# Gate and up units of three feed-forward stages: the two state halves in one 512-column product

## What is computed

```python
def _swiglu(h, w_gate, w_up, w_down):
    return (jax.nn.silu(h @ w_gate) * (h @ w_up)) @ w_down

for layer in range(DEPTH):                       # DEPTH = 2
    h = _rmsnorm(x, ffn1_norm[layer])
    x = x + 0.5 * _swiglu(h, ffn1_w_gate[layer], ffn1_w_up[layer], ffn1_w_down[layer])
    ...
    h = _rmsnorm(x, ffn2_norm[layer])
    x = x + 0.5 * _swiglu(h, ffn2_w_gate[layer], ffn2_w_up[layer], ffn2_w_down[layer])
```

## Time and profile before

| | |
|---|---|
| median of 3 runs | 1725.09 us (1724.85 to 1726.63) |
| the profiled execution's own time | 1727.27 us |
| its span, first to last instruction | 1725.4 us |
| mean granted PE clock | 0.993 of 2.4 GHz |
| PE / PEld / DVE / ACT / POOL busy | 96% / 88% / 66% / 46% / 14% |
| HBM traffic | 328 MB read, 191 GB/s over the span |

### The profile page before, as it was taken

How to read it: one execution, slowest core, us unless ns; L and a number is a source line. 1 busy time by engine, 2 the same in 40 slices (tenths; PEclk the granted TensorE clock), 3 DMA queues, 4 the chain that set the end, 5 groups by cost and what they waited for, 6 DMA issues and landing times.

```text
span 1725.4 us, 30270 instructions
## 1 busy us (share of the span) xinstructions
PE 1658.2 (96%) x12336; PEld 1523.0 (88%) x12336; DVE 1137.1 (66%) x1385; ACT 791.2 (46%) x959; POOL 233.9 (14%) x300
## 2 busy tenths in 40 slices
PE   3999899999999999999999999999999999999998
PEld 2998799988987999889998978999899999889997
DVE  7877887888677444675657886555655557555554
ACT  1655433346445343453445656343544345553433
POOL 3000100000000000068946200000000004000000
PEclk8999999999999999999999999999999999999999
DMA  9954778784644655455554424555465555335552
GB/s 320 360 199 166 250 278 315 274 288 135 217 171 150 198 190 189 155 160 194 178 187 147 148 100 154 194 180 185 154 212 170 194 179 174 112 127 194 184 194 82
DMA packets 221391, 330.23 MB, mean 191 GB/s; under 512 B 6311, under 2 KB 183048, under 8 KB 221310
## 3 DMA queue, kind: packets, MB, share of 16 engines
q1 hardware_dynamic: 206112, 276.91, 48.0%
q0 software_dynamic: 14800, 52.06, 8.6%
q10 hardware_dynamic: 398, 0.11, 0.0%
HBM read 327.97 MB, written 1.09 MB: 191 GB/s over the span
## 4 chain that ended last, share of the span: by engine, by line
PE 82%; DVE 8%; ACT 4%; DMA 3%; issue 2%; SPq 0%; ACTq 0%; DVEq 0%; POOL 0%
PE bank L2380 41%; PE bank L2422 23%; PE bank L2410 7%; DVE s_wL L1871 2%; ACT s_wH L1504 2%; DVE s_late L1889 1%; PE bank L2392 1%; DMA s_raw<-in_w_in_ab 1%; DMA s_mix<-in_w_ada 1%; PE bank L2538 1%; PE bank L2530 1%; PE bank L2529 1%; DMA s_late<-in_w_ada 1%; PE bank L2479 1%; DVE s_mix L2083 0%
## 5 line engine op out<-in xcount | busy, mean ns | idle before, releaser
L1871 DVE TENSOR_TENSOR s_wL<-s_raw,s_wH 128x2048 fp32r<-128x2048 f32 x254 | 586.4, 2313 | 306.8 <-ACT s_wH L1504 306.2
L2380 PE MATMUL bank<-s_hH,s_wH 128*128 128x256 f32 x2240 | 636.9, 284 | 10.5 <-DVE s_hL L1919 5.2
L2380 PE MATMUL bank<-s_hH,s_wL 128*128 128x256 f32 x2240 | 634.5, 283 | 0.0
L2380 PE MATMUL bank<-s_hL,s_wH 128*128 128x256 f32 x2240 | 634.5, 283 | 0.0
L1504 ACT ACTIVATE s_wH<-s_raw 128x2048 fp32r<-128x2048 f32 x254 | 484.2, 1907 | 153.5 <-PE bank L2422 115.5
L2380 PEld LDWEIGHTS bank<-s_hH,s_wH 128*128 128x128 f32 x2240 | 430.3, 192 | 15.9 <-issue 11.6
L2380 PEld LDWEIGHTS bank<-s_hL,s_wH 128*128 128x128 f32 x2240 | 430.4, 192 | 2.3 <-issue 0.2
L2380 PEld LDWEIGHTS bank<-s_hH,s_wL 128*128 128x128 f32 x2240 | 430.4, 192 | 0.0
L2422 PE MATMUL bank<-s_wH,s_aH 128*128 128x512 f32 x488 | 192.1, 394 | 2.4 <-DVE s_aL L2089 2.4
L2422 PE MATMUL bank<-s_wL,s_aH 128*128 128x512 f32 x488 | 191.2, 392 | 0.0
L2422 PE MATMUL bank<-s_wH,s_aL 128*128 128x512 f32 x488 | 190.4, 390 | 0.0
(11 more groups left out here) (456 smaller groups left out, 2130.6 us busy)
## 6 DMA issues: line engine op xcount, KB each, us to landing
s_raw<-in_w_ffn_in SPq DMA_DIRECT2D x44, 1024.0 KB, 5.8
s_raw<-in_ffn_w_gate SPq DMA_DIRECT2D x44, 1024.0 KB, 5.1
s_raw<-in_ffn_w_up SPq DMA_DIRECT2D x44, 1024.0 KB, 5.1
s_raw<-in_ffn_w_down SPq DMA_DIRECT2D x44, 1024.0 KB, 4.8
s_late<-in_w_ada POOLq DMA_DIRECT2D x20, 2048.0 KB, 10.2
s_raw<-in_w_ffn_out SPq DMA_DIRECT2D x22, 1024.0 KB, 5.0
s_raw<-in_w_in_ab SPq DMA_DIRECT2D x12, 1024.0 KB, 11.5
s_raw<-in_w_in_cd SPq DMA_DIRECT2D x12, 1024.0 KB, 6.3
```

The source lines that it names most:

```text
L1871: TTn(wL[:, slot, :], raw[:, slot, :], wH[:, slot, :].bitcast(F32), ALU.subtract).then_inc(lo_ready, 1)
L2380: last = mm(dst[:, ft * T:ft * T + T], w, h[:, k, :], start=opens(name, ft, k, i), stop=(k == KC - 1 and i == 2), skip_group_check=True)
```

## The change

In the stages f2a, f1b and f2b (`WIDE`), from chunk 1 on, the gate and up units are done by `wide_unit`. `hH` and `hL` become the two halves of one tensor `hHL`. wH is the stationary side of one product with 512 moving columns, hH and hL one after the other (two runs of 256 with 8 KB between them), into a whole bank: columns 0 to 255 take wH·hH, columns 256 to 511 wH·hL. wL·hH is a second product, of 256 columns, added to columns 0 to 255. So each half of 128 hidden columns takes a bank of its own: banks 4 and 5 for the gate, 6 and 7 for the up unit. The sum of a bank's two halves is made outside PE: ACT copies the right halves of the two banks to `low_g` or `low_u` (two copies of 128x256, `copy_low`), and DVE adds them to the left halves (two additions, `joined`).

The order of the rest changes with it. Gate: `joined` into `gsc`, then the multiplication by the row in place (`wide_scaled`). Up: `joined` into `usc`, not scaled; instead `sil` is multiplied by the row in place between two splits (`silu_scaled`), and `wide_product` multiplies `sil` by `usc`. Chunk 0 stays as it was, but its up unit goes to bank 7. f1a, ff0 and ff1 keep their instructions.

```diff
+        hHL = sb("hHL", [P, 2, KC, T], F32R)
+        hH, hL = hHL[:, 0], hHL[:, 1]
...
+        WIDE = {n: i for i, n in enumerate(["f2a", "f1b", "f2b"])}
+        low_g, low_u = t32[:, 0:2, :], t32[:, 2:4, :]
...
+            def wide_unit(slot, n, dst):
+                H, L = unit_in(slot, n)
+                for ft, k in by_halves():
+                    wh, wl = H[:, k, ft * P:ft * P + P], L[:, k, ft * P:ft * P + P]
+                    mm(dst[ft][:], wh, hHL[:, :, k, :], start=(k == 0), stop=(k == KC - 1), skip_group_check=True)
+                    last = mm(dst[ft][:, 0:T], wl, hH[:, k, :], start=False, stop=(k == KC - 1), skip_group_check=True)
+                last.then_inc(unit_used, 1)
...
+                def copy_low(low, tiles):
+                    for ft in range(2):
+                        last = A(low[:, ft, :], tiles[ft][:, T:2 * T], ACT.Copy)
+                    last.then_inc(ev("low_copied"), 1)
...
                     act_e.wait_ge(unit_used, n + (USED0 + 1))
+                    if name in WIDE:
+                        copy_low(low_g, (bank[4], bank[5]))
                     silu(i)
                     split((s + 3) % RING, n + 3, i + ((n0 + 5) // RING))
                     split((s + 4) % RING, n + 4, i + ((n0 + 6) // RING))
+                    if name in WIDE:
+                        act_e.wait_ge(unit_used, n + (USED0 + 3))
+                        copy_low(low_u, (bank[6], bank[7]))
                     hidden(i)
...
+                def joined(dst, tiles, low):
+                    for ft in range(2):
+                        last = TTn(dst[:, ft * T:ft * T + T], tiles[ft][:, 0:T], low[:, ft, :], ALU.add)
+                    return last
+                def wide_scaled(i, n):
+                    dve.wait_ge(ev("low_copied"), i * 2 + (20 * WIDE[name] - 1))
+                    joined(gsc, (bank[4], bank[5]), low_g).then_inc(u_scaled, 1)
+                    dve.wait_ge(u_scaled, i * 3 + (U0[name] - 1))
+                    TTn(halves(gsc), halves(gsc), by_row, ALU.mult).then_inc(g_scaled, 1)
+                def silu_scaled(i):
+                    dve.wait_ge(sil_done, i + (f + 1))
+                    TTn(halves(sil), halves(sil), by_row, ALU.mult).then_inc(u_scaled, 1)
+                def wide_product(i, n):
+                    dve.wait_ge(ev("low_copied"), i * 2 + 20 * WIDE[name])
+                    joined(usc, (bank[6], bank[7]), low_u).then_inc(u_scaled, 1)
+                    dve.wait_ge(u_scaled, i * 3 + (U0[name] + 1))
+                    TTn(act, sil, usc, ALU.mult).then_inc(act_mul, 1)
+                    dve.wait_ge(act_hi, i + (f + 1))
...
+                if name in WIDE:
+                    wide_scaled(FC - 1, n0 + 29)
+                    split_py(n0 + 32)
+                    silu_scaled(FC - 1)
+                    wide_product(FC - 1, n0 + 30)
```

More of the change, by code:

```diff
@@ L103, in build_program @@
         t32 = sb("t32", [P, KC, T])
-        hH = sb("hH", [P, KC, T], F32R)
-        hL = sb("hL", [P, KC, T], F32R)
+        hHL = sb("hHL", [P, 2, KC, T], F32R)
+        hH, hL = hHL[:, 0], hHL[:, 1]
         mix = sb("mix", [P, 10368])
@@ L270, in build_program @@
         RFFN = {n: i for i, n in enumerate(["f1a", "f2a", "f1b", "f2b"])}
+        WIDE = {n: i for i, n in enumerate(["f2a", "f1b", "f2b"])}
+        low_g, low_u = t32[:, 0:2, :], t32[:, 2:4, :]
+        U0 = {n: sum(11 if m not in WIDE else 31 for m in RFFN if RFFN[m] < RFFN[n]) for n in RFFN}
         ones_col = ones[:, 0:1]
@@ L1702, in ffn @@
                 act_e.wait_ge(unit_used, n0 + 29 + USED0 + 1)
+                if name in WIDE:
+                    copy_low(low_g, (bank[4], bank[5]))
                 silu(FC - 1)
                 split_py(n0 + 32)
+                if name in WIDE:
+                    act_e.wait_ge(unit_used, n0 + 30 + USED0 + 1)
+                    copy_low(low_u, (bank[6], bank[7]))
                 if name == "f1a":
@@ L2076, in product @@
                     dve.wait_ge(unit_used, n + (USED0 + 1))
-                    up = bank[5][:]
+                    up = bank[7 if name in WIDE else 5][:]
                     if name in RFFN:
-                        TTn(halves(usc), halves(bank[5][:]), by_row, ALU.mult).then_inc(u_scaled, 1)
-                        dve.wait_ge(u_scaled, i + (11 * RFFN[name] + 1))
+                        TTn(halves(usc), halves(up), by_row, ALU.mult).then_inc(u_scaled, 1)
+                        dve.wait_ge(u_scaled, i + (U0[name] + 1))
                         up = usc
@@ L2099, in body @@
                     n = i * 3 + (n0 - 1)
[L2100 to L2103, removed]
+                    if name in WIDE:
+                        wide_scaled(i, n)
+                        split((n0 + 5) % RING, n + 3)
+                        silu_scaled(i)
+                        split((n0 + 6) % RING, n + 4)
+                        wide_product(i, n + 2)
+                        TTn(aL[:], halves(act), aH[:].bitcast(F32), ALU.subtract).then_inc(act_lo, 1)
+                    else:
+                        scaled(i, n)
+                        split((n0 + 5) % RING, n + 3)
+                        split((n0 + 6) % RING, n + 4)
+                        hidden(i, n + 2)
                     split((n0 + 7) % RING, n + 5)
@@ L2118, in ffn @@
                         body(i)
-                scaled(FC - 1, n0 + 29)
-                split_py(n0 + 32)
-                product(FC - 1, n0 + 30)
+                if name in WIDE:
+                    wide_scaled(FC - 1, n0 + 29)
+                    split_py(n0 + 32)
+                    silu_scaled(FC - 1)
+                    wide_product(FC - 1, n0 + 30)
+                else:
+                    scaled(FC - 1, n0 + 29)
+                    split_py(n0 + 32)
+                    product(FC - 1, n0 + 30)
                 TTn(hL[:, 0:2, :], halves(act), hH[:, 0:2, :].bitcast(F32), ALU.subtract).then_inc(act_lo, 1)
@@ L2646, in ffn, with gate_unit, up_unit @@
                     row_bc(name)
-                cols_unit((n0 + 1) % RING, n0 + 1, bank[5])
+                cols_unit((n0 + 1) % RING, n0 + 1, bank[7 if name in WIDE else 5])
                 if name == "f1a":
                     row_bc(name)
+                def gate_unit(slot, n):
+                    if name in WIDE:
+                        wide_unit(slot, n, (bank[4], bank[5]))
+                    else:
+                        cols_unit(slot, n, bank[4])
+                def up_unit(slot, n):
+                    if name in WIDE:
+                        wide_unit(slot, n, (bank[6], bank[7]))
+                    else:
+                        cols_unit(slot, n, bank[5])
                 def body(i, turn=None, first=False):
@@ L2652, in body @@
                     gate_free(i)
-                    cols_unit((n0 + 2) % RING, n, bank[4])
+                    gate_unit((n0 + 2) % RING, n)
                     if turn:
@@ L2659, in body @@
                         turn(2)
-                    cols_unit((n0 + 4) % RING, n + 2, bank[5])
+                    up_unit((n0 + 4) % RING, n + 2)
                     if turn:
@@ L2683, in ffn @@
                 gate_free(FC - 1)
-                cols_unit((n0 + 29) % RING, n0 + 29, bank[4])
+                gate_unit((n0 + 29) % RING, n0 + 29)
                 if name == "f1a":
@@ L2687, in ffn @@
                 pe.wait_ge(act_lo, FC - 1 + f)
-                cols_unit((n0 + 30) % RING, n0 + 30, bank[5])
+                up_unit((n0 + 30) % RING, n0 + 30)
                 if with_ada:
```

## The result

| | before | after |
|---|---|---|
| median, 17 runs each | 1726.12 us (1723.59 to 1728.21) | 1729.56 us (1726.35 to 1733.76) |
| ratio | | 1.0020, 95% interval 1.0014 to 1.0027 |
| span of the profiled execution | 1725.4 us | 1728.4 us |

What follows compares the result with a forecast made beforehand. PE was taken to bound the stage, with 179.3 of 179.6 us of work. Products -11.4, stage ends +7.8 and clock +3.5 summed to -0.1 us, so 1725.0 us from the runs' median of 1725.1; range 1720.3 to 1734.3.

Steps and rivals of the forecast that it cites:

- the stage's end: Behind U(10) in three stages: longer DVE chain makes PE lose 3.08 us instead of 0.49, 7.8 us in all.
- PE's products: Gate and up units, 960 groups: three narrow products become one wide and one narrow, 11.9 ns less each, 11.4 us gained.
- the clock: Behind the stage ends' idle stretches: clock falls in two of three, 1.75 us each, 3.5 us; bounds 0 and 5.3.
- the price of the wide product: Each 512-column product in gate and up units: taken as 227.9 ns, the down products' price.
- The fixed piece: Each PE product, whatever its width: 11.9 ns, worked out as 2 x 119.9 - 227.9.
- the piece shrinks in the mixture: Rival, wide beside narrow products: gain between nothing and half of 11.4 us; with a fifth, 1734.1 us; 7%.
- The rival of two runs: Rival, each of 960 wide products: second run of 256 columns pays the fixed piece again, gain 0, 1736.4 us; 13%.
- The loop: Chunks before the stage's end: no PE wait, cost nothing; `aL` done near 3.9 us, under 5.57, 1.6 us to spare.
- The rule of the Trainium skill: PE's products: N/2.4 + 2.5 ns between products, so a piece of 2.5 ns and a gain of 2.4 us.

Runs made afterwards that it cites:

- the one with filled stretches: Changed kernel with 11 products of zeros put into PE's idle stretch at each of the three stage ends: 1726.54 us against 1725.40 before, ratio 1.0008.
- the order by twos: Changed kernel with the products of a wide unit in the order wide, wide, narrow, narrow: 1723.56 us in one run.

## Why the prediction was wrong

I had forecast no change, -0.1 us, and it was +3.4 us. The time lies inside the range, but the interval of 2.4 to 4.7 us leaves out no change: a gain that was to pay for the stage's end did not come in full. By the terms:

| term | predicted | measured |
|---|---|---|
| PE's products | -11.4 us | -5.7 us (10 x 0.19 x 3) |
| the stage's end | +7.8 us | +7.0 us (3 x 2.33) |
| the clock | +3.5 us | +2.3 us (the changed kernel less the one with filled stretches) |
| sum | -0.1 us | +3.6 us |

- **The step that failed is the price of the wide product**, "I take the down products' price, since they also alternate weight loads with 512 columns". The fixed piece I worked out from two widths is right where products of one width follow each other: the 348 ns a pair came back in the order by twos. It is not right where single wide and single narrow products alternate: it is 353 ns, which takes 5 of the 12 ns that were to be gained, and the down unit behind such units takes 5.50 instead of 5.47 us; with both, half of the gain was left. My rival "the piece shrinks in the mixture", at 7%, had the place and the bound (between nothing and half), but reckoned with a fifth of the gain. The weight load that it named as a reason is not shown. I had all the rows for a whole unit of one width and none for a mixture, and gave the mixture the sum of the two; a term that is 60 x 16 times a difference of two prices deserved its own range inside the forecast.
- **The rival of two runs falls**: laid out in one run, the product costs the same.
- **The stage's end was right in mechanism and about 10% too heavy.** From the end of G(10) at 1413.35, additions at 1.44 (1.60 worked out), last split on DVE 5.47 (5.67), additions 8.28 (8.47), `hL` 10.46 (10.64), PE 11.20 (11.39). Of the 0.2 us too much, 0.08 are that G(10) took 5.65 us and not 5.57, so that the chain behind U(9) began that much earlier against its end. The rest is a slip of mine: from a pair of additions to the next operation I had 0.87 us twice and 0.78 once, and it is 0.79. U(10) too was 0.08 us longer and covered that much more of the chain. A pair of additions took 0.75 us, a pair of copies 0.66, as taken from the nearest rows. Moving SiLU's scaling by one place gave the 0.60 us of the working.
- **The loop was right**: no wait of PE in it; `aL` was done 3.8 us after U(9)'s end (3.9 worked out), and G(10) covers 5.65.
- **The clock was right in mechanism; its size is less sure**: 3.5 against 2.3 us, with the wide interval above. It fell behind 11 of 18 stretches, near the two in three that I took, and a fall cost 1.3 to 1.6 us, not 1.75.
- **The rule of the Trainium skill** (TensorE: Matmul & The Clock Gate, Back-to-back issue gap), 2.5 ns beyond the columns, which the section gives for a single product's gap, makes 2.4 us of gain by my estimate, where 5.7 were measured and I had 11.4. But its sum, 7.8 + 3.5 - 2.4 = +8.9 us, is farther from +3.4 than mine. The traces don't agree with it: products of 256 columns in a row are 119.9 ns apart, and the 348 ns of the order by twos show the piece of 12 ns.
- **The chances**: that the sum came as near as it did is in part luck, since the products' term was 5.7 us off and the other two 2.0 us the other way. What decides between same and slower was a sum near zero of three terms of 4 to 11 us each; 55% within 0.2% was too much for that.

## What to carry to other kernels

Merging two products into one wider one saves only a product's fixed piece, so price it in the order in which the products will stand, and try grouping by width first: here the order by twos doubled what a chunk gained (0.39 us against 0.19). What is done for it on other engines was free in a loop that PE bounds and cost 2.33 us at each stage's end; keep the last one or two rounds in the old form. Here idle stretches of PE of 2.1 to 2.8 us could cost more than their length, as the clock fell behind many of them; if such a stretch can't be removed, fill it.

## What the hardware showed that was not expected

- Products of 512 and 256 columns that alternate singly take 353 ns a pair; in the order two and two and in groups of eight 348 to 349 ns. Another order of slices (352) or of banks (353) changes little. The reason stays open.
- A moving side of two runs of 256 numbers, 8 KB apart, costs no more than one run of 512 (353 ns a pair in both).
- Of kernels with the same idle stretch some executions lose clock and some don't: 11 of 18 stretches of 2.65 to 2.81 us were followed by a fall of 1.3 to 1.6 us, and three stretches that were filled with products of zeros by none.
